# Gathering tokens for two experts at once, as a rounded part and a remainder, and a gate eviction one turn later

## The reference

```python
def swiglu(h, w_gate, w_up, w_down):                       # D = 1024, D_FF = 2816
    return (jax.nn.silu(h @ w_gate) * (h @ w_up)) @ w_down

x = x + gt2 * swiglu(rms_norm(x, g_ffn[l]) * (1 + sc2) + sh2, w_gate[l], w_up[l], w_down[l])

def moe_swiglu(h, router, w_gate, w_up, w_down):
    t = h.reshape(b * s, d)
    top_val, top_idx = lax.top_k((t @ router).astype(jnp.float32), TOP_K)      # 2 of 8
    top_w = jax.nn.softmax(top_val, axis=-1)
    gates = jnp.sum(jax.nn.one_hot(top_idx, N_EXPERTS) * top_w[..., None], axis=1)
    out = jnp.zeros_like(t)
    for e in range(N_EXPERTS):
        out = out + gates[:, e:e + 1] * swiglu_2(t, w_gate[e], w_up[e], w_down[e])
    return out.reshape(b, s, d)
```

## Time and profile before

| | |
|---|---|
| median of three runs | 2608.47 us |
| the profiled execution's own time | 2608.57 us |
| its span | 2606.7 us, mean granted TensorE clock 0.942 |
| TensorE, VectorE, ScalarE, GpSimd busy | 92%, 67%, 51%, 7% |
| read from HBM | 539 MB, 207 GB/s over the span |
| gated feed-forwards | about 250 to 470, 550 to 770 and 950 to 1155 us |
| routing | about 1757 to 1768 us |
| walk over the 8 jobs | about 1778 to 2602 us |

### The profile page before, as it was taken

How to read it: one execution, slowest core, us unless ns; L and a number is a source line. 1 busy time by engine, 2 the same in 40 slices (tenths; PEclk the granted TensorE clock), 3 DMA queues, 4 the chain that set the end, 5 groups by cost and what they waited for, 6 DMA issues and landing times. The chain is left out here.

```text
span 2606.7 us, 44497 instructions
## 1 busy us (share of the span) xinstructions
PE 2398.8 (92%) x17191; PEld 2178.3 (84%) x17191; DVE 1755.1 (67%) x2849; ACT 1326.7 (51%) x2083; POOL 185.3 (7%) x168
## 2 busy tenths in 40 slices
PE   7898999889988989979789997788999999999998
PEld 5787899679878779979689986567999999999997
DVE  3556555555565455566655566548999999999997
ACT  2343434433443544443344442336777777777775
POOL 0500000000005000008100003000000000000000
PEclk9899999989998989989789997778999999999999
DMA  8524465155633045534034551026999999999995
GB/s 344 198 98 178 185 228 202 65 209 220 229 137 130 15 159 189 178 130 162 17 136 181 193 192 65 1 89 262 342 335 343 342 341 337 335 343 334 334 346 205
DMA packets 82228, 542.86 MB, mean 208 GB/s; under 512 B 9328, under 2 KB 9840, under 8 KB 33904
## 3 DMA queue, kind: packets, MB, share of 16 engines
q1 hardware_dynamic: 79184, 529.57, 54.8%
q10 hardware_dynamic: 2848, 10.55, 1.1%
HBM read 539.03 MB, written 1.05 MB: 207 GB/s over the span
## 5 line engine op out<-in xcount | busy, mean ns | idle before, releaser
L827 PE MATMUL bank<-w_hi,src_hi 128*128 128x256 f32 (+1 forms) x2320 | 672.3, 290 | 15.7 <-DVE src_lo L598 6.3
L3267 DVE TENSOR_TENSOR w_lo<-ring,w_hi 128x1024 fp32r<-128x1024 f32 x528 | 636.1, 1219 | 46.3 <-ACT w_hi L3196 33.4
L828 PE MATMUL bank<-w_lo,src_hi 128*128 128x256 f32 (+1 forms) x2320 | 663.7, 286 | 0.0
L829 PE MATMUL bank<-w_hi,src_lo 128*128 128x256 f32 (+1 forms) x2320 | 662.5, 286 | 0.0
L827 PEld LDWEIGHTS bank<-w_hi,src_hi 128*128 128x128 f32 x2320 | 448.7, 193 | 35.3 <-issue 24.7
L828 PEld LDWEIGHTS bank<-w_lo,src_hi 128*128 128x128 f32 x2320 | 449.8, 194 | 7.2
L829 PEld LDWEIGHTS bank<-w_hi,src_lo 128*128 128x128 f32 x2320 | 449.5, 194 | 0.7
L827 PE MATMUL bank<-src_hi,w_hi 128*128 128x256 f32 x1472 | 427.2, 290 | 12.1 <-DVE w_lo L1170 8.9
L1170 DVE TENSOR_TENSOR w_lo<-ring,w_hi 128x1024 fp32r<-128x1024 f32 x260 | 317.9, 1223 | 170.3 <-ACT w_hi L1098 170.2
L828 PE MATMUL bank<-src_lo,w_hi 128*128 128x256 f32 x1472 | 422.3, 287 | 0.0
L829 PE MATMUL bank<-src_hi,w_lo 128*128 128x256 f32 x1472 | 422.0, 287 | 0.0
(11 more groups left out here) (432 smaller groups left out, 2783.9 us busy)
## 6 DMA issues: line engine op xcount, KB each, us to landing
ring<-in_moe SPq DMA_DIRECT2D x176, 1024.0 KB, 7.1
ring<-in_ffn SPq DMA_DIRECT2D x66, 1536.0 KB, 6.6
ring<-in_moe SPq DMA_DIRECT2D x176, 512.0 KB, 6.8
ring<-in_ffn_ev SPq DMA_DIRECT2D x22, 1536.0 KB, 6.5
oT<-in_w_ada SPq DMA_DIRECT2D x20, 1024.0 KB, 6.5
big<-in_w_ada SPq DMA_DIRECT2D x20, 1024.0 KB, 8.5
ring<-in_w_in SPq DMA_DIRECT2D x18, 1024.0 KB, 6.4
ring<-in_w_out SPq DMA_DIRECT2D x12, 1024.0 KB, 5.0
```

The costliest lines, as they stand in the source:

```text
L827: pe.matmul(out, ah, bh, start=start and i == 0, stop=False, skip_group_check=True)
L828: pe.matmul(out, ah, bl, start=False, stop=False, skip_group_check=True)
L829: mm = pe.matmul(out, al, bh, start=False, stop=stop and i == n - 1, skip_group_check=True)
L3267: dve.tensor_tensor(wl, piece, wh.bitcast(F32), ALU.subtract).then_inc(p.w_lo[kind].sem, 1)
```

## The change

Three things, in the diff below.

1. In the feed-forwards with a gate, `spread_act` stands at the end of ScalarE's turn 2 instead of turn 1.
2. The tokens are gathered for two experts at once. Picks, sources and the walk's loop go by pairs: TensorE gathers during the odd jobs only, in four parts at turns 12, 13, 14 and 17, for both jobs of the next pair. `xn` is split once, in `route`, into a rounded part `xnH` (ScalarE) and a remainder `xnL` (VectorE), and a gather is 32 fp32r products of 128 weights against 256 columns (2 chunks of features x 2 tiles of tokens x 2 parts of `xn`, four times). The pick is written as fp32r; its ones and zeros are exact. Two sets of sources alternate between pairs.
3. The walk has jobs 0 to 2 written out, jobs 3 to 6 as the body of a loop that runs once or three times, and job 7 after it.

```diff
@@ ffn, ScalarE
-                if c == 1 and gate is not None:
+                if c == 2 and gate is not None:
                     spread_act(p, act, p.gates[:, 1, :])
@@ route, ScalarE
             act.activation(share, less, ACT.Exp).then_inc(ex.sem, 1)
+            act.wait_ge(*p.sig("gained")(1))
+            for t in range(NT):
+                act.activation(p.xnH[:, t, :], p.xn[:, t, :], ACT.Copy).then_inc(p.sig("xn_hi").sem, 1)
@@ route, VectorE, ahead of the wait for the counts
+            for t in range(NT):
+                dve.wait_ge(*p.sig("xn_hi")(t + 1))
+                ins = dve.tensor_tensor(p.xnL[:, t, :], p.xn[:, t, :], p.xnH[:, t, :].bitcast(F32), ALU.subtract)
+            chain(ins)
             dve.wait_ge(*counted(1))
@@ moe
-    S_BANK, G_BANK = (6, 7, 5, 6), (5, 6)
+    GATHER_AT = (12, 13, 14, 17)
+    S_BANK, G_BANK = (6, 7, 5, 6), (5, 6, 7, 5)
+    sources = ((p.srcH, p.srcL), (p.srcH2, p.srcL2))
@@ walk
-        for b in range(NE - 3):
+        for b in range(NE - 5):
...
-            for b in (NE - 3, NE - 2):
+            for b in range(NE - 5, NE - 1):
@@ TensorE
-                pe.wait_ge(*job_at(picked, i, 1, j + 1))
-                for k in range(4 * part, 4 * part + 4):
+                pe.wait_ge(*job_at(picked, i, 1, j + 2))
+                if part == 3:
+                    pe.wait_ge(*job_at(job_lo, i, 2, 2 * j + 1))
+                for k in range(2 * part, 2 * part + 2):
                     for t in range(NT):
-                        mm = pe.matmul(p.ps[G_BANK[part]][:, (k % 4) * P:(k % 4) * P + P], xn[:, t, k * P:k * P + P],
-                                       pick[:, j % 2, t, :], start=t == 0, stop=t == NT - 1)
+                        for v in (p.xnH, p.xnL):
+                            mm = pe.matmul(p.ps[G_BANK[part]][:, (k % 2) * T:(k % 2) * T + T], v[:, t, k * P:k * P + P],
+                                           pick[:, j // 2 % 2, t, :], start=t == 0 and v is p.xnH,
+                                           stop=t == NT - 1 and v is p.xnL)
...
-                if 12 <= r < 14 and not last:
-                    if not first:
-                        pe.wait_ge(*job_at(added, i, 4, 4 * b))
-                    gather(i, b + 1, r - 12)
+                if r in GATHER_AT and b % 2 and not last:
+                    pe.wait_ge(*job_at(added, i, 4, 4 * b))
+                    gather(i, b + 1, GATHER_AT.index(r))
@@ ScalarE
-                if 15 <= r < 17 and not last:
-                    keep_job(i, b + 1, r - 15)
+                if r - 3 in GATHER_AT and b % 2 and not last:
+                    keep_job(i, b + 1, GATHER_AT.index(r - 3))
@@ VectorE
-                for t in range(NT):
-                    job = slice(j, j + 1) if isinstance(i, int) else bass.ds(i * 2 + j, 1)
-                    ins = dve.tensor_scalar(pick[:, j % 2, t, :], iota, p.slot[:, t, job], None, ALU.is_equal)
-                ins.then_inc(picked.sem, 1)
+                for m in range(2):
+                    job = slice(j + m, j + m + 1) if isinstance(i, int) else bass.ds(i * 4 + (j + m), 1)
+                    for t in range(NT):
+                        ins = dve.tensor_scalar(pick[:, j // 2 % 2, t, m * P:m * P + P], iota, p.slot[:, t, job], None,
+                                                ALU.is_equal)
+                    ins.then_inc(picked.sem, 1)
...
-                if r == 6 and not last:
-                    if not first:
-                        dve.wait_ge(*job_at(wt_turned, i, 1, b))
+                if r == 6 and b % 2 and not last:
+                    dve.wait_ge(*job_at(wt_turned, i, 1, b))
                     make_pick(i, b + 1)
-                if 16 <= r < 18 and not last:
-                    keep_rest(i, b + 1, r - 16)
+                if r - 4 in GATHER_AT and b % 2 and not last:
+                    keep_rest(i, b + 1, GATHER_AT.index(r - 4))
```

More of the change, by code:

```diff
@@ L2987, in _ @@
             chain(dve.tensor_copy(p.trip[:, 0:1], most))
-            chain(dve.tensor_scalar(most, most, -3.0, None, ALU.add))
+            chain(dve.tensor_scalar(most, most, 0.5, -1.0, ALU.mult, ALU.add))
             dve.tensor_copy(p.trip[:, 1:2], most).then_inc(routed.sem, 1)
@@ L3002, in moe @@
     DOWN = 2
-    xn = p.xn
-    big, work = p.big, p.work
-    pick = big[:, 0:512].rearrange("p (b t s) -> p b t s", b=2, t=NT)
+    work = p.work
+    pick = p.pick
     WT, yH, yL = p.pickT[:], p.yH[:], p.yL[:]
@@ L3048, in walk @@
         for r in range(FC + 3):
-            step(between, NE - 3, r, False, True)
+            step(between, NE - 5, r, False, True)
     def there(r, lag, first):
@@ L3095, in up @@
                 hs = slice((k // FC % 2) * P, (k // FC % 2) * P + P)
+                srcH, srcL = sources[k // FC // 2 % 2]
                 for half in range(2):
@@ L3138, in step @@
                 if r == 0:
-                    pe.wait_ge(*job_at(job_lo, i, 2, 2 * b + 2))
+                    pe.wait_ge(*job_at(job_lo, i, 2, 2 * (b - b % 2) + 4))
                 if r < FC:
@@ L3161, in step @@
                         scatter(i, b, q)
-            pe.wait_ge(*p.sig("gained")(1))
-            gather(0, 0, 0)
-            gather(0, 0, 1)
+            for part in range(4):
+                gather(0, 0, part)
             walk(pe, between, step)
@@ L3169, in _ @@
         def _(act):
[L3170 removed]
+            between = act.value_load(p.trip[0:1, 1:2], min_val=1, max_val=3)
             def keep_job(i, j, part):
                 act.wait_ge(*job_at(gathered, i, 2, 2 * j + part + 1))
[L3175 to L3177 removed]
+                act.activation(sources[j // 2 % 2][0][:, 2 * part:2 * part + 2, :].rearrange("p k s -> p (k s)"),
+                               p.ps[G_BANK[part]][:, :], ACT.Copy).then_inc(job_hi.sem, 1)
             def keep_output(i, j):
@@ L3221, in step @@
                     keep_output(i, b)
-            for part in range(2):
+            for part in range(4):
                 keep_job(0, 0, part)
@@ L3228, in _ @@
         def _(dve):
-            between = dve.value_load(p.trip[0:1, 1:2], min_val=1, max_val=5)
+            between = dve.value_load(p.trip[0:1, 1:2], min_val=1, max_val=3)
             iota = p.con_at(CON2, "iota")
             def make_pick(i, j):
-                for t in range(NT):
-                    job = slice(j, j + 1) if isinstance(i, int) else bass.ds(i * 2 + j, 1)
-                    ins = dve.tensor_scalar(pick[:, j % 2, t, :], iota, p.slot[:, t, job], None, ALU.is_equal)
-                ins.then_inc(picked.sem, 1)
+                for m in range(2):
[4 more added lines that the diff above has]
+                    ins.then_inc(picked.sem, 1)
             def keep_rest(i, j, part):
                 dve.wait_ge(*job_at(job_hi, i, 2, 2 * j + part + 1))
-                ks, ss = slice(4 * part, 4 * part + 4), slice((j % 2) * P, (j % 2) * P + P)
-                dve.tensor_tensor(p.srcL[:, ks, ss], p.ps[G_BANK[part]][:, :].rearrange("p (k s) -> p k s", k=4),
-                                  p.srcH[:, ks, ss].bitcast(F32), ALU.subtract).then_inc(job_lo.sem, 1)
+                high, low = [v[:, 2 * part:2 * part + 2, :].rearrange("p k s -> p (k s)") for v in sources[j // 2 % 2]]
+                dve.tensor_tensor(low, p.ps[G_BANK[part]][:, :], high.bitcast(F32), ALU.subtract).then_inc(job_lo.sem, 1)
             def add_scattered(i, j, q):
@@ L3249, in add_scattered @@
                 dve.wait_ge(*job_at(scattered, i, 4, 4 * j + q + 1))
-                job = slice(j, j + 1) if isinstance(i, int) else bass.ds(i * 2 + j, 1)
+                job = slice(j, j + 1) if isinstance(i, int) else bass.ds(i * 4 + j, 1)
                 dve.scalar_tensor_tensor(out=x, in0=p.ps[S_BANK[q]][:, :], scalar=p.weight[:, t, job], in1=x,
```

25 lines of the change are left out of this document (16 added, 9 removed).

## The result

The changed kernel takes 2576.57 us (median of four runs, 2575.21 to 2581.67) against 2607.76 us of the kernel before beside it: ratio 0.9881, 95% interval 0.9868 to 0.9893. The forecast was 2584.0 us, the range 2578 to 2595. The time lies 1.4 us under the range. The profiled execution took 2575.79 us, its span is 2574.0 us.

A forecast was written before the change was run, and what follows sets the result against it. TensorE was taken to set the pace, busy 92% of the span, with VectorE 7% behind in the walk. 2608.6 - 13.65 (feed-forwards) - 13.6 (walk) + 2.6 (ahead of the walk) = 2584.0 us, range 2578 to 2595.

The forecast's parts named there:

- The feed-forwards' idle time and low clock: Turn 2 of three gated feed-forwards: 2.98 us TensorE wait and 1.57 us low clock go, 13.65 us saved in all.
- rival A: Gated feed-forwards: the idle time goes but the clock doesn't come back, 2588.7 us; chance 0.05.
- B: Gated feed-forwards: the stall moves to turn 2's end, losing all 13.65 us, 2597.6 us; chance 0.05.
- The walk: Expert walk: seven gathers removed (25.1 us), three two-job gathers added (11.5 us), 13.6 us saved.
- C: Walk's even jobs: VectorE becomes the pace, they don't shorten, 14.3 us lost, 2598.3 us; chance 0.04.
- D: Walk: transfers capped at their 332 GB/s mean, so it can't shorten, +13.6 us, 2597.6 us; chance 0.03.
- E: Walk's job starts, turn 2 to 3: stalls grow, slower than before, 2616 us at 3 us on seven; chance 0.03.
- The head: Ahead of the walk: added roundings, remainders, picks and the first gather cost +2.6 us, bounds 1.5 and 4.1.
- The sign that the prediction named, the walk's first product: Start of the walk: its first product comes 2.6 us later behind the last product of the layer before.
- 2608.6 - 13.65 - 13.6 + 2.6: Whole kernel: profiled time less feed-forward and walk savings, plus the cost ahead of the walk, giving 2584.0 us.
- about 4 between runs: Whole kernel: allowance for differences between runs in the range's lower end, 2578 us.
- the two theories: Experiments, untouched parts: 1, change worth its forecast, rest chance; 2, clock level follows the parts' starting moment, so it repeats.

The follow-up runs named there:

- e12: The changed kernel a third time, no edit: 2581.98 us, ratio 0.9899.
- e4: The kernel before again, no edit: 2608.75 us, ratio 1.0002.
- e8: The kernel before with a pause (VectorE memset of 1536 columns) ahead of the second layer's part: 2607.62 us, ratio 1.0.
- e3: The changed kernel again, no edit: 2580.56 us, ratio 0.9889.
- e1: The kernel before with only the gate eviction moved to turn 2: 2590.15 us, ratio 0.9925.
- e10: The changed kernel with VectorE's two remainders behind the first picks, rounded part's product lost for some features of the first pair: 2578.12 us, ratio 0.9885.
- e11: e10 with 23 TensorE products added whose results nobody reads, in the routing and around the first gather: 2579.29 us, ratio 0.9895.

## Why the prediction was right in its parts and short in its sum

- *The feed-forwards' idle time and low clock.* Right. -4.55, -4.26 and -5.83 us in the first profile, -4.49, -4.25 and -4.84 in e12, for -4.55 each. The clock came back, so rival A fell, and nothing waits at turn 2's end, so B fell. That the first is -4.55 to the hundredth is luck: over the nine profiles with the move it is 4.1 to 5.1 us. The third is some 0.3 to 1.3 us over its size. Its part has 21.7 us at the low level before, 16.8 in e12 and 12.4 in the first profile, so the extra 1 us there is again the clock's course.
- *The walk.* Right: -13.2 to -13.6 us for -13.6, in all nine profiles with the new gather (791.5 to 791.9 us). In the first profile the gather's products stand 117 ns apart and its turns take 5.25 to 5.30 us; in all nine, even jobs take 98.75 to 98.90 us, odd ones 102.50 to 102.86 (job 0 aside, whose first turns differ). The even jobs' late turns stay at 4.34 us with VectorE 97% busy and 362 GB/s: C and D fell. The prediction's own evidence against D was weaker than it said: 362 GB/s is what a turn's pieces come to, but job 7's ten turns moved 285 GB/s in the trace (window 2541.45 to 2584.87 us), since the last pieces had been fetched ahead (62 GB/s in its last two turns). E needs waits at the job starts that are longer by 1.9 us or more; the longest is 0.9 us, where it was 0.8.
- *The head.* Right, 0.3 us too small. The sign that the prediction named, the walk's first product, comes 2.9 us later for 2.6: the slots 1.95 us later (2.0 forecast), and 18 of the gather's 32 products ran at the low level where it took 16. The table's +1.6 is less because the first turn behind it had low clock in the first profile of before (7.28 us) and not in e4 (5.99), against which the head is +2.9 as well. e8, with the old gather, has a head of 38.33 us, so the whole head by itself says little.
- *The step that failed* is in the sum: "2608.6 - 13.65 - 13.6 + 2.6". It prices everything that isn't touched at nothing. In the course of the first profile those parts gave 9.3 us, in that of e12 and e3 0.1 to 0.2. The clock was considered only where the edits act, in turn 2 (with rival A) and in the first gather; that low stretches elsewhere move when something ahead of them changes stood in no rival, and the range had only "about 4 between runs" for it. The reported four runs lay mostly on the quick side: all 12 runs give 26.6 us saved for 24.6 forecast, and their median, 2581.7 us, lies inside the range. What sets on which side an execution falls is open.

Open: which courses there are, and whether a part's start or the idle time ahead of it sets them. In e1, e10 and e11 the parts from 1339 to 1749 us are 2.9 to 3.0 us shorter than before, in the first profile, e3 and e12 they are not. Of the two theories, 1 was wrong in that executions with the same course agree within 0.1 us in most parts, and 2 in that one kernel has several courses.

## What to carry to other kernels

Where an engine's queue, worked in order, stands behind another engine's late result, move the wait to where the result is old. The worth is the idle time plus the low clock behind it, and both can be read ahead of time from two turns side by side. When a kernel has stretches at a lower granted clock, give every difference an allowance for untouched parts with such stretches (here 9 us of 2600 in one course and none in another), and check it after by windows over parts with the same instruction counts before crediting a mechanism. A change of less than this allowance needs several profiles of each kernel, compared part by part.

## What the runs showed of the hardware

- A pause of 2.26 us ahead of a part of 50.41 us made the part 2.14 us shorter with the same instructions (e8), at a granted clock of 0.92 for 0.87. The totals with a pause (2607.81 and 2607.62 us for 2607.84, and 2582.32 for 2581.98) can't tell whether the whole pays for its pause.
- Where the clock takes the same course, lengths of parts repeat from one execution to another: within 0.05 us between before and e4 from 251 to 1749 us, within 0.1 between e3 and e12 from 548 to 1749, though the first 251 us differ by up to 5 us.
- One part of 788 TensorE instructions took 120.6, 124.6 to 124.7, or 123.4 to 123.8 us in 14 profiles, with 5.07 or 5.08, 4.88 to 5.06, or 14.2 to 14.6 us left of a low stretch at its start.
- In the changed kernel's walk TensorE was busy for 43.00 of 43.00 us, some ten turns, with transfers at 362 GB/s and VectorE 97% busy.
- Two GpSimd subtractions of 128x1024 (2.35 us each) held two small VectorE instructions for 1.3 and 1.8 us; the others in the same stretch took their usual time.
